# Splitting the first two weight slots of each stage by row block, and moving the sums of squares

## The reference

```
y = x * rsqrt(mean(x * x) + eps) * w          # norm over the width 1024
h = y @ w_in                                  # [256 or 272, 1024] @ [1024, n]
FFN:  (silu(h_gate) * h_up) @ w_down          # width 2816
x = x + (0.5 or 1) * part
```

## Time and profile before

| | us |
|---|---|
| median of 3 runs | 1618.59 |
| range of the runs | 1618.41 to 1620.3 |
| the profiled execution, its own time | 1617.96 |
| its span in the profile | 1616.2 |
| TensorE matmul busy | 1518.0 (94%) |
| VectorE busy | 1097.8 (68%) |
| ScalarE busy | 768.5 (48%) |
| GpSimd busy | 90.6 (6%) |
| mean HBM rate | 152 GB/s |

### The profile page before, as it was taken

How to read it: one execution, slowest core, us unless ns; L and a number is a source line. 1 busy time by engine, 2 the same in 40 slices (tenths; PEclk the granted TensorE clock), 3 DMA queues, 4 the chain that set the end, 5 groups by cost and what they waited for, 6 DMA issues and landing times.

```text
span 1616.2 us, 26076 instructions
## 1 busy us (share of the span) xinstructions
PE 1518.0 (94%) x10408; PEld 1355.4 (84%) x10408; DVE 1097.8 (68%) x1341; ACT 768.5 (48%) x1012; POOL 90.6 (6%) x84
## 2 busy tenths in 40 slices
PE   7999999788999999999977899999999979999997
PEld 6888899788888888888866888888988867878886
DVE  6877578664678767776566577856656665678764
ACT  6554368633544444544445454445254433454532
POOL 2000200100000010000100000003022010000001
PEclk9999999998999999999979999999999999999999
DMA  8554665310365556655631346366453322555551
GB/s 283 169 194 143 208 198 158 112 55 2 131 192 177 174 180 200 196 171 170 213 128 53 130 157 198 122 220 208 129 153 105 105 79 79 183 168 171 174 182 58
DMA packets 243967, 247.47 MB, mean 153 GB/s; under 512 B 4993, under 2 KB 242321, under 8 KB 243889
## 3 DMA queue, kind: packets, MB, share of 16 engines
q1 hardware_dynamic: 242112, 242.89, 47.0%
q0 software_dynamic: 1056, 2.30, 0.4%
q10 hardware_dynamic: 720, 1.17, 0.2%
HBM read 245.30 MB, written 1.05 MB: 152 GB/s over the span
## 4 chain that ended last, share of the span: by engine, by line
PE 78%; DVE 10%; ACT 7%; issue 3%; DMA 1%; POOL 0%; SPq 0%; ACTq 0%; DVEq 0%; POOLq 0%
PE ps L335 37%; PE ps L336 19%; ACT whi L299 4%; DVE wlo L305 3%; PE ps L339 2%; PE ps L340 2%; PE ps L341 2%; PE ps L1854 2%; PE ps L1855 2%; PE ps L1856 2%; PE ps L1119 1%; PE ps L1878 1%; PE ps L1866 1%; PE ps L2019 1%; PE ps L436 1%
## 5 line engine op out<-in xcount | busy, mean ns | idle before, releaser
L335 PE MATMUL ps<-u,whi 128*128 128x512 f32 x1744 | 617.2, 398 | 11.5 <-DVE u L405 11.5
L305 DVE TENSOR_TENSOR wlo<-raw,whi 128x2048 fp32r<-128x2048 f32 (+3 forms) x260 | 532.7, 2080 | 123.3 <-ACT whi L299 123.3
L336 PE MATMUL ps<-u,wlo 128*128 128x256 f32 x1744 | 493.3, 283 | 0.0
L299 ACT ACTIVATE whi<-raw 128x2048 fp32r<-128x2048 f32 (+3 forms) x260 | 438.0, 1721 | 56.6 <-PE ps L336 44.7
L335 PEld LDWEIGHTS ps<-u,whi 128*128 128x128 f32 x1744 | 330.1, 189 | 88.6 <-DVE u L405 12.8
L336 PEld LDWEIGHTS ps<-u,wlo 128*128 128x128 f32 x1744 | 332.0, 190 | 0.2
L335 PE MATMUL ps<-h,whi 128*128 128x512 f32 x880 | 308.1, 394 | 0.0
L336 PE MATMUL ps<-h,wlo 128*128 128x256 f32 x880 | 247.5, 281 | 0.0
L335 PEld LDWEIGHTS ps<-h,whi 128*128 128x128 f32 x880 | 165.4, 188 | 38.1
L336 PEld LDWEIGHTS ps<-h,wlo 128*128 128x128 f32 x880 | 166.1, 189 | 0.0
L339 PE MATMUL ps<-u,whi 128*128 128x256 f32 (+1 forms) x488 | 142.2, 291 | 5.4 <-DVE u L631 2.9
(11 more groups left out here) (363 smaller groups left out, 2102.9 us busy)
## 6 DMA issues: line engine op xcount, KB each, us to landing
raw<-in_ffn_w_gu SPq DMA_DIRECT2D x87, 1024.0 KB, 5.7
raw<-in_ffn_w_down SPq DMA_DIRECT2D x32, 768.0 KB, 5.4
raw<-in_w_in SPq DMA_DIRECT2D x22, 1024.0 KB, 5.3
raw<-in_ffn_w_down SPq DMA_DIRECT2D x32, 640.0 KB, 4.7
raw<-in_a_w_in SPq DMA_DIRECT2D x16, 1024.0 KB, 5.9
raw<-in_w_ffn_gate SPq DMA_DIRECT2D x11, 1024.0 KB, 5.4
raw<-in_w_ffn_up SPq DMA_DIRECT2D x11, 1024.0 KB, 6.3
raw<-in_b_w_in SPq DMA_DIRECT2D x6, 1024.0 KB, 7.2
```

The source lines that it names most:

```text
L299: nc.scalar.activation(whi[:, s, 0:n], raw[:, s, 0:n], ACT.Copy).then_inc(w_hi, 1)
L305: nc.vector.tensor_tensor(wlo[:, s, 0:n], raw[:, s, 0:n], whi[:, s, 0:n].bitcast(F32), ALU.subtract).then_inc(w_lo, 1)
L335: nc.tensor.matmul(o, whi[:, s, w], both, start=(first and k == 0), stop=False)
L336: ins = nc.tensor.matmul(o[:, 0], wlo[:, s, w], both[:, 0], start=False, stop=(last and k == nk - 1))
```

## The change

- A new `stage_opening` is used by every stage from A on, apart from N. TensorE runs all column blocks of the first slot with row blocks 0 to 5 (12 steps; 6 in A), then waits for the second slot and for `x` being complete (`s_x`, because the second slot's PSUM banks can be those of the last output pair), runs the second slot with row blocks 0 to 5 (12 steps; 6 in A, where only one column block of the second slot is taken here), waits for the last `ulo`, runs row blocks 6 and 7 of the first slot, then `sums`, then row blocks 6 and 7 of the second slot. In A the second column block of the second slot follows.
- In F0 the sums follow the second slot.
- In the FFN stages the wait for the root moves from ahead of the third slot to between the third and the fourth.

The matmuls are the same in number and shape.

```diff
--- before.py
+++ after.py
@@ -450,9 +450,39 @@
             ins.then_inc(w_used, 1)
             pe.wait_ge(l_ones, 48)
 
-        def x_split(st):
-
-            return s_ulo, 4 * split_no(st), 2
+        def stage_opening(pe, st, first, second, between=None):
+
+
+            tok, n, early = QT, 4 * split_no(st), KB - 2
+
+            def part(g, outs, k0, k1, waits=False):
+                s = g % SLOTS
+                for b, o in enumerate(outs):
+                    for k in range(k0, k1):
+                        if waits and b == 0 and k % 2 == 0:
+                            pe.wait_ge(s_ulo, n + k // 2 + 1)
+                        wide = slots[g][4]
+                        w = slice(k * wide + b * P, k * wide + b * P + P)
+                        if len(o.shape) == 3:
+                            nc.tensor.matmul(o, whi[:, s, w], u2[:, k, :, tok], start=(k == 0), stop=False)
+                            ins = nc.tensor.matmul(o[:, 0], wlo[:, s, w], uhi[:, k, tok], start=False, stop=(k == KB - 1))
+                            continue
+                        nc.tensor.matmul(o, whi[:, s, w], uhi[:, k, tok], start=(k == 0), stop=False)
+                        nc.tensor.matmul(o, whi[:, s, w], ulo[:, k, tok], start=False, stop=False)
+                        ins = nc.tensor.matmul(o, wlo[:, s, w], uhi[:, k, tok], start=False, stop=(k == KB - 1))
+                return ins
+
+            (g, outs), (g1, outs1) = first, second
+            pe.wait_ge(w_lo, MORE + g + 1)
+            part(g, outs, 0, early, waits=True)
+            pe.wait_ge(w_lo, MORE + g1 + 1)
+            pe.wait_ge(s_x, 4 * norm_no["N" if st == "R" else st] + 4)
+            part(g1, outs1, 0, early)
+            pe.wait_ge(s_ulo, n + 4)
+            part(g, outs, early, KB).then_inc(w_used, 1)
+            if between:
+                between()
+            return lambda: part(g1, outs1, early, KB)
 
         def sums(pe, st):
             add_squares(pe, st, False)
@@ -495,7 +525,7 @@
         def glu_banks(u):
             return 4 * (u % 2)
 
-        def glu_products(pe, st, u, i=None, between=None, ready=None):
+        def glu_products(pe, st, u, i=None, between=None):
 
             g, tok, b0 = first_slot[st] + 2 * u, tok_of[st], glu_banks(u)
             per = 4 if i is not None else 0
@@ -503,10 +533,7 @@
 
                 pe.wait_ge(s_up, UNITS * ffn_no[st] + u + (2 * i if i is not None else 0))
             rhs = (u2,)
-            if g == 0 and i is None:
-                first_blocks(pe)
-            else:
-                slot_blocks(pe, g, [halves(b0 + b) for b in range(2)], rhs, i=i, per=per, tok=tok, ready=ready)
+            slot_blocks(pe, g, [halves(b0 + b) for b in range(2)], rhs, i=i, per=per, tok=tok)
             if between:
                 between()
             slot_blocks(pe, g + 1, [halves(b0 + 2 + b) for b in range(2)], rhs, i=i, per=per, tok=tok)
@@ -679,11 +706,17 @@
 
         def ffn_pe(pe, st):
             g0, tok, nxt = first_slot[st], tok_of[st], next_of(st)
-            glu_products(pe, st, 0, between=lambda: sums(pe, st), ready=x_split(st))
-            pe.wait_ge(s_std, norm_no[st] + 1)
+            if st == stages[0]:
+                first_blocks(pe)
+                slot_blocks(pe, g0 + 1, [halves(2 + b) for b in range(2)], (u2,), tok=tok)
+                sums(pe, st)
+            else:
+                rest = stage_opening(pe, st, (g0, [halves(b) for b in range(2)]), (g0 + 1, [halves(2 + b) for b in range(2)]),
+                                     between=lambda: sums(pe, st))
+                rest().then_inc(w_used, 1)
             with pe.Fori(0, UNITS // 2) as i:
-                for j in range(2):
-                    glu_products(pe, st, 1 + j, i)
+                glu_products(pe, st, 1, i, between=lambda: pe.wait_ge(s_std, norm_no[st] + 1))
+                glu_products(pe, st, 2, i)
             gd, n0 = g0 + 2 * UNITS, UNITS * ffn_no[st]
 
             pe.wait_ge(s_up, n0 + UNITS)
@@ -995,6 +1028,14 @@
 
             steps = (len(L_LEVELS) + 1) * AG
 
+            def block_b(g, o):
+                for k in range(KB):
+                    w = slice(k * WIDE + P, k * WIDE + 2 * P)
+                    nc.tensor.matmul(o, whi[:, g % SLOTS, w], uhi[:, k, tok], start=(k == 0), stop=False)
+                    nc.tensor.matmul(o, whi[:, g % SLOTS, w], ulo[:, k, tok], start=False, stop=False)
+                    ins = nc.tensor.matmul(o, wlo[:, g % SLOTS, w], uhi[:, k, tok], start=False, stop=(k == KB - 1))
+                return ins
+
             def turn_y(i):
                 if i < AG:
                     pe.wait_ge(sa["y0"], i + 1)
@@ -1016,13 +1057,15 @@
                             ins = nc.tensor.matmul(ps[r, bank, o], a_Y[r, n], ident[r, r], start=True, stop=True)
                 ins.then_inc(sa["yt"], 1)
 
-            for m in range(17):
+            rest = stage_opening(pe, "A", (g0, [a_bank(0)[:, 0]]), (g0 + 1, [a_bank(1)[:, 0]]), between=lambda: sums(pe, "A"))
+            for m in range(1, 17):
                 if m >= 3:
                     pe.wait_ge(sa["in"], m - 2)
-                outs = [a_bank(m)[:, b] for b in range(1 if m == 0 else 2)]
-                slot_blocks(pe, g0 + m, outs, (uhi, ulo), tok=tok, ready=x_split("A") if m == 0 else None)
-                if m == 0:
-                    sums(pe, "A")
+                if m == 1:
+                    rest()
+                    block_b(g0 + 1, a_bank(1)[:, 1]).then_inc(w_used, 1)
+                else:
+                    slot_blocks(pe, g0 + m, [a_bank(m)[:, b] for b in range(2)], (uhi, ulo), tok=tok)
                 if m == 2:
 
                     pe.wait_ge(sa["in"], 1)
@@ -1564,12 +1607,9 @@
                 if ks[-1] == KB - 1:
                     ins.then_inc(w_used, 1)
 
-            for m in range(3):
-                b0 = (0, 2, 5)[m]
-                slot_blocks(pe, g0 + m, [ps[:, b0 + b, 0:SEQ] for b in range(2)], (uhi, ulo), tok=tok,
-                            ready=x_split("B") if m == 0 else None)
-                if m == 0:
-                    sums(pe, "B")
+            outs = [[ps[:, b0 + b, 0:SEQ] for b in range(2)] for b0 in (0, 2, 5)]
+            stage_opening(pe, "B", (g0, outs[0]), (g0 + 1, outs[1]), between=lambda: sums(pe, "B"))().then_inc(w_used, 1)
+            slot_blocks(pe, g0 + 2, outs[2], (uhi, ulo), tok=tok)
             pe.wait_ge(sbn["bias"], 4)
             pe.wait_ge(s_std, norm_no["B"] + 1)
             for t in range(2):
@@ -1897,11 +1937,14 @@
                     pe.wait_ge(sr["in"], m - 2)
                 b0 = in_bank(m)
                 tm = in_tok(m)
-                slot_blocks(pe, g0 + m, [ps[:, b0 + b, tm] for b in range(slots[g0 + m][4] // P)], (uhi, ulo), tok=tm,
-                            ready=x_split("R") if m == 0 else None)
+                outs = [ps[:, b0 + b, tm] for b in range(slots[g0 + m][4] // P)]
                 if m == 0:
-                    sums(pe, "N")
-                    sums(pe, "R")
+                    outs1 = [ps[:, 2 + b, tm] for b in range(2)]
+                    rest = stage_opening(pe, "R", (g0, outs), (g0 + 1, outs1), between=lambda: (sums(pe, "N"), sums(pe, "R")))
+                elif m == 1:
+                    rest().then_inc(w_used, 1)
+                else:
+                    slot_blocks(pe, g0 + m, outs, (uhi, ulo), tok=tm)
                 if m == 1:
                     pe.wait_ge(sr["tab"], LR)
                     pe.wait_ge(s_std, norm_no["R"] + 1)
```

## The result

The changed kernel takes 1604.39 us in the median of 4 runs (1603.32 to 1605.58), the kernel before 1619.34 of 4 (1618.41 to 1620.3). The ratio is 0.9908, with a 95% interval from 0.9891 to 0.9925. The profiled execution took 1603.47 us with a span of 1601.7, against 1617.96 and 1616.2: 14.5 us less span, where the prediction's sum had 14.4. The median lies 0.2 us from the forecast 1604.2 and well inside the range of 1599.8 to 1608.9.

What follows compares the result with a forecast made beforehand. TensorE, busy for 94% of the span, bounds the kernel; time is won only where it waits or runs at the lower clock. 16.2 + 0.6 + 0 - 2.8 + 0.4 = 14.4 us gives 1604.2 us, range 1599.8 to 1608.9.

Steps and rivals of the forecast that it cites:

- FFN openings, 16.2 us: Openings of F1 to F4: waits for the last `ulo` and the clock's fall go, gaining 2.7 + 1.5 + 5.5 + 6.5 us.
- The chain behind the sums in FFN stages: Sums to the fifth slot's rest, worked out for F1: later sums cost nothing, with 1.7 us of slack.
- the slower rival: Rival, chance 0.04: the root's chain binds in every FFN stage, at the fifth slot's rest; 1621.7 us.
- F0, 0.6 us: F0's second slot goes ahead of the sums, which wait for GpSimd's fold; gain between 0 and 0.9 us, taken as 0.6.
- A, 0: A's opening: the 1.2 us wait goes, but 1.4 us comes ahead of the third slot; gain 0, between -0.5 and +1.4.
- B, -2.8: B's first scores come 16.5 us after the sums, now 2.8 us later; loss 2.8 us, bounds +1.5 and -3.8.
- R, +0.4: R's first turn comes 2.0 us earlier, but the clock falls behind a 2.6 us wait; gain 0.4, between 0.4 and 2.0.
- The sum: Whole kernel: the terms of the FFN openings, F0, A, B and R add up to a gain of 14.4 us.
- Hidden chains: Rival, chance 0.12: the chains in B and R are hidden after all; gain 18.8 us, time 1599.8.
- The clock staying low elsewhere: Rival, chance 0.12: waits in A, B and F4 bring new falls of the clock; gain 10.2 us, time 1608.4.
- New waits in place of the old: Rival, chance 0.07: the second slot can't start behind 12 steps, so 2.1 us per wait is covered; 1611.0 us.

Runs made afterwards that it cites:

- The run with 12 steps: Changed kernel, but F1 to F4 open with the 12 steps of their own first slot alone, the second slot undivided after the sums; 1606.65 us.
- the run with the longer chain: Changed kernel with two unused reciprocals added on VectorE between the root and its reciprocal in every FFN stage; 1611.57 us.
- the run with the early rest: Changed kernel, but in A VectorE makes the third slot's rest ahead of its wait for the table load and the reciprocal; 1600.95 us.
- the two B runs: Changed kernel with only B edited: back to its old opening (1601.23 us), or opening with its own first slot, then the sums (1599.41 us).

## Why the prediction was right, step by step

**FFN openings, 16.2 us.** Right: 2.7, 1.5, 5.4 and 6.3 measured. The wait for `x` in F4 was 0.26 us for the 0.3 taken, and 0.5 us with its restart. That F3 and F4 owe part to the clock is read from the kernel before: of F3's 12.17 us only 3.75 were idle, and 5.5 were lost. The run with 12 steps agrees: with a wait of 1.65 us and the clock at 1.00, F3 loses 1.8 us.

**The chain behind the sums in FFN stages.** Right: hidden. The up addition came 3.7 us after the third slot's start (4 was forecast). The slack was 1.7 in the sum. In F1 of the changed kernel (reciprocal, third slot, up addition, the split of two slots with the fifth slot's first, fifth slot):

```profile
434.05 1.75 DVE L502 RECIPROCAL rstd<-std 128x256 f32<-128x256 f32 x1 [1.25 <-ACT std L496]
434.75 0.39 PE L335 MATMUL ps<-u,whi 128*128 128x512 f32 x1
...
438.44 0.69 DVE L566 TENSOR_TENSOR up_s<-ps,up_s 128x512 f32<-128x512 f32 x1 [1.18 <-ACT up_s L553]
...
441.69 4.49 DVE L305 TENSOR_TENSOR wlo<-raw,whi 128x2048 fp32r<-128x2048 f32 x2
...
445.95 0.39 PE L335 MATMUL ps<-u,whi 128*128 128x512 f32 x1
```

One split is half of 4.49 us, so it ends at 443.94 and the slack is 445.95 - 443.94 = 2.0 us; it was 2.1 by the run with the longer chain. Past that, the slower rival begins: there 1.4 of the 3.5 us added were lost in each stage, once. No run moves the wait for the root back. In F1 it would not have held TensorE, since the root is done by 434.05 and the third slot starts at 434.75; in F0 the root ended at 27.5 and the third slot started at 26.66, so there it would have.

**F0, 0.6 us.** The order of events was right, a wait of 2.8 us for the slot in place of 4.2 for the fold. F0 gained 1.1 us in this trace, but the size is not settled: the first 28 us differ by more than that from execution to execution. The slack of the chain was 0.7 us where the sum had 0.2.

**A, 0.** Right for the opening: the wait moved to the third slot, 1.29 us for 1.4 forecast, and the run with the early rest removes it. That A is 0.6 us longer was not forecast; the eight traces with this order have A at 221.2 to 223.9 us.

**B, -2.8.** The mark was right to 0.01 us (26.49 for 26.5). The loss of the stage was mis-sized: 1.2 us in this trace. The 2.8 us were still whole 44.5 us into the stage; half of them came back where the clock stayed up behind a wait of 1.9 us at which the kernel before had lost it. Before, and with the old opening, the clock fell there and B was 113.0 us long both times. Of seven traces with the late scores it fell there in one, in which B was 116.3 us long; in the others B was 113.7 to 114.3.

**R, +0.4.** The turn came 1.9 us earlier for 2.0, behind a wait of 2.59 for 2.6, and the clock fell as taken. At the later wait, 165 us into R, 0.2 us of that were left for the 0.4 forecast. Two of the nine traces with this mark kept the clock behind the turn; they are at that place after 163.6 and 163.7 us instead of 165.2 to 165.3, so the fall costs 1.6 us, as taken, and the other end of the forecast's bounds, a gain of 1.9 for 2.0, is there as well. Here is one of them, behind its turn:

```profile
1117.39:1122.39 5.00, 5.00 (x37) 1.00 0.13 25
```

The whole stage was 0.7 us longer all the same, because of what came behind 165 us; over the nine traces it was 304.8 to 309.1 us.

**The sum.** That 14.4 met 14.5 is in part luck. B came out 1.6 us and F0 0.5 us better than forecast, R 1.1, A 0.6 and the FFN openings 0.3 us worse, and these errors cancel. What is shown by marks is the path at each opening, not the total to a tenth of a microsecond.

**Rivals.** Hidden chains: refuted in B by the two B runs, and in R by the run with R's sums earlier, whose turn kept its 6.85 us behind them. The clock staying low elsewhere: it fell in R, as forecast, and not at A's moved wait nor at F4's for `x`; B as a whole had a mean granted clock of 0.93, above the 0.89 of before. New waits in place of the old: only 0.3 us in F4. Slower: refuted at this size.

## What to carry to other kernels

When work is reordered so that TensorE has something to do while an operand is late, ask at once what else it puts off: here a few matmuls for a norm, whose result a serial chain of two other engines awaits. Put in front of them just as many steps as the late operand needs (12 in B and F2, 24 in F3 and F4), not the same number everywhere. Where a stall at an opening is removed and the time doesn't move, read which slot or product TensorE waits for next and what stands ahead of it in its maker's list.

## What the runs showed of the hardware

One and the same wait can cost the clock or not. R's first turn waited 2.59 or 2.60 us in nine traces; in the 5 us behind it the granted clock was 0.66 in seven of them and 1.00 in two. In F1 2.41 us left it at 1.00, ahead of line 1081 2.31 us dropped it; at that place with the early rest 1.78 and 1.86 us left it up and 1.91 us was followed by a fall. No wait of 1.3 us did so at an opening. This agrees with what the Trainium skill says in "TensorE: Matmul & The Clock Gate", what's actually happening, that the gate's period runs free of the kernel. A, B and R are full of waits of such lengths, and with equal marks they differ by 2.6 to 4.4 us between traces (A 221.2 to 223.9, B 113.7 to 116.3, R 304.8 to 309.1). The mean granted clock over R was 0.99 where it took 304.8 us and 0.97 where it took 309.1. F1 and F2, which have no such wait, come out at 186.1 us in every trace of a kernel that left them unedited. So a change of 1 us in a mixer is to be read from marks, not from the total.
